# Order of the low parts at three stage changes, and the entry and head changes of the latent attention, in a two-block fp32 kernel on one core

## The chip, the core and the metric

The kernel runs on one core of a Trainium2 chip. A core has five engines that run their own instruction streams and meet at semaphores: TensorE (PE, matrix products into PSUM), VectorE (DVE), ScalarE (ACT), GpSimd (POOL) and SyncE (SP, which only issues transfers here). The metric is device microseconds of one execution; lower is better.

## What is computed

Two blocks in a row on 512 tokens of width 1024. The first has two layers: a mixer, a layer norm, a squared-ReLU MLP, a layer norm. The mixer of layer 0 is a gated delta rule, that of layer 1 a gated linear attention. The second block is a latent attention with a pooling branch.

```python
def first_block(x, ...):
    for i in range(DEPTH):                       # DEPTH = 2
        m = _mixer_gdn(x, ...) if i % 2 == 0 else _mixer_gla(x, ...)
        x = _layernorm(DEEPNORM_ALPHA * x + m, ln1_g[i], ln1_b[i])
        x = _layernorm(DEEPNORM_ALPHA * x + _sq_relu_mlp(x, mlp_w1[i], mlp_w2[i]), ln2_g[i], ln2_b[i])
    return x

# second block: h is the normed, modulated x; hc the same of the 256 context tokens
    u = h @ w_in[l];  uc = hc @ w_in[l]
    q, k, v = _mla_qkv(u, ...);  qc, kc, vc = _mla_qkv(uc, ...)   # 4 heads of 128 + 64 rotary, values 128 wide
    attn = _attend(q, concat(kc, k), concat(vc, v))               # softmax over 768 keys
    y = _branches(u, attn, w_pool[l], pool_scale[l]) @ w_out[l]   # silu gates, multiscale pooling
    x = x + gate * y
```

## The kernel before

**Large products.** Every weight and activation of the large products is split into a high part (a copy in the type fp32r, made by ACT) and a low part (the value less the high part, made by DVE). A product is then three fast products: high by high, high by low, low by high (`mm3`, L280 to L282). Weights come in slabs of 128x2048 in two halves: SP loads a half into `raw`, ACT makes `whi` (`split_hi`, L253), DVE makes `wlo` (`split_lo`, L259) and frees `raw` by the semaphore `w_ready`, on which the next load waits. PE runs one slab after another.

**The three stage changes.** The token layers `a_out`, `down0` and `b_out` each end in sums of 128 tokens (tiles 0 to 3), which must be normed and turned before `up0`, `b_qk` and `up1` can begin. DVE runs `dve_token_end`: per tile it adds the sum to `X` (L428), takes statistics (L436, L438), and, when ACT has made the root (L455, L457), centres (L447) and scales (L450) the tile, tile 3 in two halves of its columns. PE turns a tile by transposes (L395), four per half tile; ACT copies the turned half into `act_hi` (L412) and DVE subtracts it into `act_lo` (L420), both for each half tile. Before, the low parts of tile 0 stand inside tile 2's norm, those of tile 1 inside tile 3's norm (between its statistics and its centring), those of tiles 2 and 3 at the end. ACT runs `act_token_end` in a like order. PE enters the next stage in `pe_feature_first`: it waits for the low parts of tile 1, then multiplies the first two tiles with output column block 0 (`part(0, ...)`, 24 products of 256 columns), with the two half turns of tile 3 in between, then with column block 1 (another 24), and then waits for the low parts of tile 3.

**The entry of the latent attention.** At the end of `pe_c_in` six value products of 512 columns are made (L2583; each runs as two passes, so a trace has two records of it), alternately in PSUM banks 6 and 7. ACT copies the even ones out (L2715) and DVE the odd ones (L2752), so the third product waits for the copy of the first, and so on, and the first score waits for all copies. Ahead of its copies ACT runs the two halves of a `split_hi` of a slab of the last layer's weights, and DVE the two halves of its `split_lo`.

**The attention.** `pe_c_attend` makes 16 steps n, four per head, in a fixed order: the scores of step n + 1 (L2834, L2835), a piece of the preparation of the next head's keys and queries (L2600, L2604, L2590, L2595, L2608), the value product of step n - 1 (L2854), the transposes of the probabilities of step n (L2843). DVE does a step's softmax (L2972, L2974, L2976, which scales by the reciprocal), the maxima for the next (L2963, L2966), and copies turned probabilities (L2982); ACT the exponentials (L2910) and the larger copies (L2918). In the third step of a head DVE makes, after the maxima, three operands of the next head in a row: rotary queries (L2759), scaled keys `kn` (L2764), scaled rotary keys `kr` (L2765). The first score of a head waits for `kr`. POOL adds squares (L2773, L2777) and runs the pooling (L2789 to L2797) beside this.

PE's queue and all others run strictly in the order written. What is built is not chosen by a planner.

Of the kernel before, what the change touches and what calls it, by code (L numbers as in the profile page):

```python
# [16 lines left out]
ALU = mybir.AluOpType  # L17
# [91 lines left out]
def build(nc, a, out):  # L109

    ctx = ExitStack()
    with ctx:
# [134 lines left out]
        def split_hi(act, k, b):  # L247
            for hf in range(2):
                act.wait_ge(raw_loaded[hf], k * 32 + (16 * b + 16))
                if hf == 0 and not (isinstance(k, int) and k == 0):  # L250
                    act.wait_ge(slab_used, k * 2 + (b - 1))
                hs = slice(hf * SLAB // 2, (hf + 1) * SLAB // 2)
                nc.scalar.activation(whi[b][:, hs], raw[hf][:, :], ACT.Copy).then_inc(w_hi_ready, 1)  # L253
# [162 lines left out]
        def dve_turned(dve, e, st):  # L416
            for hf in range(2):
                dve.wait_ge(act_hi_ready, 8 * e + 2 * st + hf + 1)
                c = (slice(None), slice(4 * hf, 4 * hf + 4), slice(st * P, st * P + P))
                nc.vector.tensor_tensor(act_lo[c], bk[TURN_BANK[st] + hf][:, :].rearrange("p (k s) -> p k s", k=4),  # L420
                                        act_hi[c], ALU.subtract).then_inc(act_ready, 1)
# [55 lines left out]
        def act_token_end(act, name, e):  # L477
            nxt = next_pair(name, PH[name][1] // 2 - 1)
            split_first_hi(act, nxt)
            act_norm_tile(act, e, 0)  # L480
            for st in range(1, ST):
                act_norm_tile(act, e, st)
                act_turned(act, e, [st - 1])
            act_turned(act, e, [3])
            split_hi(act, nxt, 1)

        def dve_token_end(dve, name, e):
            nxt = next_pair(name, PH[name][1] // 2 - 1)
            split_first_lo(dve, nxt, [0])
            dve_norm_tile(dve, name, e, 0, lambda: split_first_lo(dve, nxt, [1]))  # L490
            dve_norm_tile(dve, name, e, 1)
            dve_norm_tile(dve, name, e, 2, lambda: dve_turned(dve, e, 0))
            dve_norm_tile(dve, name, e, 3, lambda: dve_turned(dve, e, 1))
            dve_turned(dve, e, 2)
            dve_turned(dve, e, 3)
            split_lo(dve, nxt, 1)
# [1085 lines left out]
        def pe_feature_first(pe, name, before, e, middle=None):  # L1582
# [12 lines left out]
            for hf in range(2):  # L1595
                pe.wait_ge(w_ready, 2 * PH[name][0] + hf + 1)
                part(0, range(4 * hf, 4 * hf + 4), 0, 2)
                pe_turn_half(pe, e, before, 3, hf)
            part(1, range(0, 8), 0, 2)
# [668 lines left out]
        def lst(*parts):  # L2268
# [3 lines left out]
                                  ("qt kn kr nrs", 1), ("v", 3), ("qt kn kr nrs", NH - 1)))  # L2272
# [250 lines left out]
        def pe_c_in(pe):  # L2523
# [52 lines left out]
            pe.wait_ge(V.sem, V.at("qt", 0))  # L2576
            pe.wait_ge(K.sem, K.at("lnq", 0))
            for t in range(6):
                if t in (2, 4):
                    pe.wait_ge(K.sem, K.at("v", t // 2 - 1))  # L2580
                if t in (3, 5):
                    pe.wait_ge(V.sem, V.at("v", t // 2 - 1))
                T.inc(nc.tensor.matmul(bk[6 + t % 2][:, :].rearrange("p (h n) -> p h n", h=NH), c_ckv[:, t * P:t * P + P], wv,  # L2583
                                       start=True, stop=True), "v")
            pe.wait_ge(K.sem, K.at("v", 2))
            pe.wait_ge(V.sem, V.at("v", 2))
# [69 lines left out]
        def act_c_in(act):  # L2656
# [55 lines left out]
            split_hi(act, next_pair("c_in", 3), 1)  # L2712
            for t in (0, 2, 4):
                act.wait_ge(T.sem, T.at("v", t))
                K.inc(nc.scalar.activation(c_v[:, t, :], bk[6][:, :], ACT.Copy), "v")  # L2715
# [5 lines left out]
        def dve_c_in(dve):  # L2721
# [25 lines left out]
            dve_c_keys(dve, 0)  # L2747
            dve_c_scale_column(dve, 0)
            split_lo(dve, next_pair("c_in", 3), 1)
            for t in (1, 3, 5):  # L2750
                dve.wait_ge(T.sem, T.at("v", t))
                V.inc(nc.vector.tensor_copy(c_v[:, t, :], bk[7][:, :]), "v")  # L2752
# [8 lines left out]
        def dve_c_keys(dve, g):  # L2761
            dve.wait_ge(K.sem, K.at("expk", g))
            kn, kr = HC[g % 2]["kn"], HC[g % 2]["kr"]
            V.inc(nc.vector.tensor_tensor(kn, kn, c_rsk, ALU.mult), "kn")  # L2764
            V.inc(nc.vector.tensor_tensor(kr, c_kr, c_rsk, ALU.mult), "kr")  # L2765
# [100 lines left out]
        def pe_c_attend(pe):  # L2866
            pe_c_score(pe, 0)
            for n in range(NB):
                g, qt = n // ST + 1, n % ST
                if n + 1 < NB:  # L2870
                    pe_c_score(pe, n + 1)
                if NB - ST - 1 <= n < NB - 1:
# [47 lines left out]
        def act_c_attend(act):  # L2920
            for n in range(NB):
# [6 lines left out]
                if n == NB - 1:  # L2928
                    for i in range(1, 7):
                        act_c_mix(act, i)  # L2930
                if g == NH:
                    continue
# [62 lines left out]
        def dve_c_attend(dve):  # L2995
            dve_c_max(dve, 0)
            for n in range(NB):
                g, qt = n // ST + 1, n % ST
                dve_c_softmax(dve, n)
# [4 lines left out]
                if qt == 2 and g < NH:  # L3004
                    dve_c_rope(dve, g, 7)
                    dve_c_keys(dve, g)
# [7 lines left out]
                dve_c_turned(dve, n)  # L3014
                if qt == 2 and g < NH:
                    dve_c_scale_column(dve, g)
# [168 lines left out]
```

## Time and profile before

| | us |
|---|---|
| median of 3 runs | 1873.69 |
| lowest, highest | 1873.48, 1875.39 |
| the profiled execution | 1872.41 |
| its span in the trace | 1870.4 |

| engine | busy, us | share |
|---|---|---|
| PE (matmul) | 1820.5 | 97% |
| DVE | 986.4 | 53% |
| ACT | 733.7 | 39% |
| POOL | 235.6 | 13% |

The profiled execution takes 2.0 us more than its span, and 1.3 us less than the median. In the trace's rows "idle before" stands in square brackets with what ended it. PE's clock is given as a share: 1.00 is 2.4 GHz and 0.50 is 1.2 GHz. Its mean over the span is 0.993.

### The profile page before, as it was taken

The page shows a single profiled execution, that of the slowest core. Times are in us where ns is not written, and L with a number is a line of the kernel's source. Part 1 is how long each engine was busy: PE and PEld are TensorE (multiplying, and loading weights), DVE is VectorE, ACT ScalarE, POOL GpSimd, SP SyncE. Part 2 cuts the span into 40 slices and gives each one's busy share as a digit, 9 for nine tenths or more (in the row PEclk, how much of TensorE's full clock was granted, in tenths as well). Part 3 has the DMA queues.
Part 4 walks back from the last instruction along what each step waited for, and adds up shares of the span by engine and source line. Part 5 has one row for each costly group of instructions (what it writes and reads, how often), then busy time and mean ns, then how long its engine had stood idle before and what let it go on. Part 6 is the DMA issues. An engine that isn't in the chain of part 4 may idle for free.

```text
span 1870.4 us, 24188 instructions
## 1 busy us (share of the span) xinstructions
PE 1820.5 (97%) x9152; PEld 1471.2 (79%) x9152; DVE 986.4 (53%) x1393; ACT 733.7 (39%) x1209; POOL 235.6 (13%) x230
## 2 busy tenths in 40 slices
PE   8999999999999999999999999999999998999999
PEld 6887798888788888887777787888888887875667
DVE  5775466666554453356321577744443567323663
ACT  4344455554232232333443444222223355334340
POOL 2001234342000001000000253000000000201500
PEclk9999999999999999999999999999999999999999
DMA  5323100000342234222222200442235222421001
GB/s 157 90 90 112 46 2 1 1 1 1 122 148 90 90 90 149 90 90 90 68 91 68 68 1 23 129 164 90 90 112 180 90 90 79 149 70 45 1 1 68
DMA packets 102374, 146.77 MB, mean 78 GB/s; under 512 B 4977, under 2 KB 70721, under 8 KB 102032
## 3 DMA queue, kind: packets, MB, share of 16 engines
q1 hardware_dynamic: 95472, 121.45, 20.5%
q0 software_dynamic: 6816, 24.13, 3.9%
q8 instruction: 59, 0.97, 0.2%
q14 instruction: 27, 0.22, 0.0%
HBM read 143.47 MB, written 2.10 MB: 78 GB/s over the span
## 4 chain that ended last, share of the span: by engine, by line
PE 91%; DVE 3%; issue 2%; ACT 2%; POOL 1%; DMA 1%; SPq 0%; ACTq 0%; DVEq 0%; POOLq 0%
PE bk L280 23%; PE bk L282 23%; PE bk L281 23%; PE bk L1092 2%; PE bk L1110 2%; PE bk L2834 1%; PE bk L2835 1%; PE bk L1101 1%; PE bk L2854 1%; PE bk L990 1%; POOL work L1512 1%; PE bk L1973 1%; PE bk L1008 1%; PE bk L1121 1%; PE bk L1152 1%
## 5 line engine op out<-in xcount | busy, mean ns | idle before, releaser
L259 DVE TENSOR_TENSOR wlo<-raw,whi 128x1024 fp32r<-128x1024 f32 x214 | 253.4, 1224 | 376.9 <-ACT whi L253 373.2
L280 PE MATMUL bk<-act_hi,whi 128*128 128x512 f32 x960 | 384.0, 400 | 0.3 <-DVE wlo L723 0.3
L281 PE MATMUL bk<-act_lo,whi 128*128 128x512 f32 x960 | 380.6, 396 | 0.0
L282 PE MATMUL bk<-act_hi,wlo 128*128 128x512 f32 x960 | 380.5, 396 | 0.0
L253 ACT ACTIVATE whi<-raw 128x1024 fp32r<-128x1024 f32 x214 | 216.1, 1053 | 265.5 <-PE bk L282 248.8
L280 PE MATMUL bk<-whi,act_hi 128*128 128x512 f32 x768 | 308.6, 402 | 2.5 <-DVE act_lo L473 1.8
L281 PE MATMUL bk<-wlo,act_hi 128*128 128x512 f32 x768 | 304.8, 397 | 0.0
L282 PE MATMUL bk<-whi,act_lo 128*128 128x512 f32 x768 | 304.7, 397 | 0.0
L280 PEld LDWEIGHTS bk<-act_hi,whi 128*128 128x128 f32 x960 | 180.5, 188 | 48.9 <-issue 4.1
L282 PEld LDWEIGHTS bk<-act_hi,wlo 128*128 128x128 f32 x960 | 180.5, 188 | 44.5
L281 PEld LDWEIGHTS bk<-act_lo,whi 128*128 128x128 f32 x960 | 180.6, 188 | 44.4 <-issue 1.0
L280 PEld LDWEIGHTS bk<-whi,act_hi 128*128 128x128 f32 x768 | 145.5, 189 | 38.9 <-issue 3.1
L282 PEld LDWEIGHTS bk<-whi,act_lo 128*128 128x128 f32 x768 | 145.3, 189 | 36.1
L281 PEld LDWEIGHTS bk<-wlo,act_hi 128*128 128x128 f32 x768 | 145.4, 189 | 34.6 <-issue 0.5
L1633 DVE TENSOR_TENSOR arena<-arena (+1 forms) x64 | 44.3, 692 | 182.2 <-ACT arena L1616 182.2
L1616 ACT ACTIVATE arena<-bk 128x512 f32 (+1 forms) x64 | 38.3, 598 | 245.2 <-PE bk L282 245.2
L1942 POOL TENSOR_TENSOR work<-work,arena 128x512 f32<-128x512 f32 x24 | 37.5, 1583 | 381.3 <-ACT work L1926 355.5
L473 DVE TENSOR_TENSOR act_lo<-arena,act_hi 128x2048 fp32r<-128x2048 f32 x32 | 73.3, 2292 | 18.8 <-ACT act_hi L467 18.8
L829 DVE SCALAR_TENSOR_TENSOR work<-work,convw 128x512 f32<-128x512 f32 x96 | 64.6, 743 | 0.0
L467 ACT ACTIVATE act_hi<-arena 128x2048 fp32r (+1 forms) x32 | 60.9, 1904 | 6.3 <-PE bk L282 6.3
L1092 PE MATMUL bk<-work 128*128 128x128 f32 x384 | 61.1, 280 | 1.3 <-DVE work L1433 1.2
L1440 DVE TENSOR_TENSOR work<-bk,work 128x256 f32<-128x256 f32 x96 | 40.6, 424 | 36.5 <-PE bk L1092 34.9
(392 smaller groups left out, 2500.8 us busy)
## 6 DMA issues: line engine op xcount, KB each, us to landing
raw<-in_mlp_w SPq DMA_DIRECT2D x128, 512.0 KB, 4.2
raw<-in_a_w_in SPq DMA_DIRECT2D x32, 512.0 KB, 4.0
work<-in_w_mod POOLq DMA_DIRECT2D x24, 512.0 KB, 4.1
raw<-in_b_w_in SPq DMA_DIRECT2D x24, 512.0 KB, 3.8
raw<-in_w_in SPq DMA_DIRECT2D x14, 512.0 KB, 4.0
raw<-in_a_w_out SPq DMA_DIRECT2D x8, 512.0 KB, 4.2
raw<-in_b_w_out SPq DMA_DIRECT2D x8, 512.0 KB, 4.0
raw<-in_w_out SPq DMA_DIRECT2D x8, 512.0 KB, 3.9
```

Of the source, the lines that this page charges most:

```text
L253: nc.scalar.activation(whi[b][:, hs], raw[hf][:, :], ACT.Copy).then_inc(w_hi_ready, 1)
L259: nc.vector.tensor_tensor(wlo[b][:, hs], raw[hf][:, :], whi[b][:, hs], ALU.subtract).then_inc(w_ready, 1)
L280: nc.tensor.matmul(acc, lhs_hi, rhs_hi, start=first, stop=False, skip_group_check=True)
L281: nc.tensor.matmul(acc, lhs_hi, rhs_lo, start=False, stop=False, skip_group_check=True)
L282: return nc.tensor.matmul(acc, lhs_lo, rhs_hi, start=False, stop=last, skip_group_check=True)
L467: nc.scalar.activation(stage(act_hi, b), hid_group(pair, b), ACT.Copy).then_inc(stage_hi_ready, 1)
L473: nc.vector.tensor_tensor(stage(act_lo, b), hid_group(pair, b), stage(act_hi, b), ALU.subtract).then_inc(stage_ready, 1)
L829: nc.vector.scalar_tensor_tensor(out=acc, in0=src, scalar=wk, in1=acc, op0=ALU.mult, op1=ALU.add).then_inc(conv_step, 1)
L1092: mm = nc.tensor.matmul(bk[s][:, c % 2 * P:c % 2 * P + P], A["K"][:, c, :], z_right(l, c * P, P), start=True, stop=True, skip_group_check= ...
L1440: nc.vector.tensor_tensor(A["T"][:, 2 * s:2 * s + 2, :], chunks(bk[s])[:, 0:2, :], A["negpair"][:, l, :].unsqueeze(1).broadcast_to([P, 2, ...
L1616: nc.scalar.activation(head_tile(hid, k2 * 4, 2 * b + j), bk[2 * b + j][:, :], ACT.Relu).then_inc(acc_free, 1)
L1633: nc.vector.tensor_tensor(tile, tile, tile, ALU.mult).then_inc(hid_ready, 1)
```

## The change

1. `dve_token_end` puts both low parts of tile 1 ahead of tile 3's norm, and the first low part of tile 2 inside it. `act_token_end` makes the high parts of tile 2 before the root of tile 3. `pe_feature_first` runs all of column block 0 first, and puts the two half turns of tile 3 behind the first and the second half of column block 1.
2. The six value products go to banks 2, 3, 6, 7, 4, 5, without waits for copies. The waits for the copies go to the attention's first step: for the first two copies ahead of its score of step 1, for all ahead of the next head's key product. The splits of the last layer's second slab leave the entry: each half stands at the end of an attention step, half 0 at step 3 and half 1 at step 7, on ACT and on DVE.
3. The scaling of the next head's keys, `kn`, goes ahead of the softmax of a head's third step; `kr` stays behind the rotary queries. `V`, the list of DVE's counted steps, is changed to match.

```diff
@@ act_token_end
             act_norm_tile(act, e, 0)
-            for st in range(1, ST):
+            for st in (1, 2):
                 act_norm_tile(act, e, st)
                 act_turned(act, e, [st - 1])
+            act_turned(act, e, [2])
+            act_norm_tile(act, e, 3)
             act_turned(act, e, [3])
@@ dve_token_end (dve_turned and split_hi get an argument that picks halves)
             dve_norm_tile(dve, name, e, 2, lambda: dve_turned(dve, e, 0))
-            dve_norm_tile(dve, name, e, 3, lambda: dve_turned(dve, e, 1))
-            dve_turned(dve, e, 2)
+            dve_turned(dve, e, 1)
+            dve_norm_tile(dve, name, e, 3, lambda: dve_turned(dve, e, 2, (0,)))
+            dve_turned(dve, e, 2, (1,))
             dve_turned(dve, e, 3)
@@ pe_feature_first
                 part(0, range(4 * hf, 4 * hf + 4), 0, 2)
+            for hf in range(2):
+                part(1, range(4 * hf, 4 * hf + 4), 0, 2)
                 pe_turn_half(pe, e, before, 3, hf)
-            part(1, range(0, 8), 0, 2)
@@ pe_c_in, its end
             pe_c_query_sum(pe, 0, 7)
-            pe.wait_ge(V.sem, V.at("qt", 0))
-            pe.wait_ge(K.sem, K.at("lnq", 0))
             for t in range(6):
-                if t in (2, 4):
-                    pe.wait_ge(K.sem, K.at("v", t // 2 - 1))
-                if t in (3, 5):
-                    pe.wait_ge(V.sem, V.at("v", t // 2 - 1))
-                T.inc(nc.tensor.matmul(bk[6 + t % 2][:, :].rearrange("p (h n) -> p h n", h=NH), c_ckv[:, t * P:t * P + P], wv,
+                if t == 0:
+                    pe.wait_ge(acc_free, 2 * FS["c_in"] + 16)
+                elif t == 2:
+                    pe.wait_ge(V.sem, V.at("qt", 0))
+                elif t == 3:
+                    pe.wait_ge(K.sem, K.at("lnq", 0))
+                elif t == 4:
+                    pe.wait_ge(K.sem, K.at("lnk", 1))
+                T.inc(nc.tensor.matmul(bk[V_BANK[t]][:, :].rearrange("p (h n) -> p h n", h=NH), c_ckv[:, t * P:t * P + P], wv,
                                        start=True, stop=True), "v")
-            pe.wait_ge(K.sem, K.at("v", 2))
-            pe.wait_ge(V.sem, V.at("v", 2))
+        V_BANK = (2, 3, 6, 7, 4, 5)
@@ act_c_in, its end
             act_c_query_norm(act, 0)
-            split_hi(act, next_pair("c_in", 3), 1)
             for t in (0, 2, 4):
@@ dve_c_in, its end
-            dve_c_keys(dve, 0)
+            dve_c_key_scaled(dve, 0)
+            dve_c_key_rope(dve, 0)
             dve_c_scale_column(dve, 0)
-            split_lo(dve, next_pair("c_in", 3), 1)
             for t in (1, 3, 5):
@@ pe_c_attend
                 g, qt = n // ST + 1, n % ST
+                if n == 0:
+                    pe.wait_ge(K.sem, K.at("v", 0))
+                    pe.wait_ge(V.sem, V.at("v", 0))
                 if n + 1 < NB:
                     pe_c_score(pe, n + 1)
+                if n == 0:
+                    pe.wait_ge(K.sem, K.at("v", 2))
+                    pe.wait_ge(V.sem, V.at("v", 2))
@@ act_c_attend
+                if n in (3, 7):
+                    split_hi(act, next_pair("c_in", 3), 1, (n // ST,))
                 if g == NH:
@@ dve_c_attend
+                if qt == 2 and g < NH:
+                    dve_c_key_scaled(dve, g)
                 dve_c_softmax(dve, n)
...
                 if qt == 2 and g < NH:
                     dve_c_rope(dve, g, 7)
-                    dve_c_keys(dve, g)
+                    dve_c_key_rope(dve, g)
...
                 dve_c_turned(dve, n)
+                if n in (3, 7):
+                    split_lo(dve, next_pair("c_in", 3), 1, (n // ST,))
```

**DVE at the end of `b_out`**, from the scaling of tile 2 (L450, 128x1024) to the last low parts (L420). Before:

```order
L450 SCALAR_TENSOR_TENSOR X<-X,rstd,work 128x1024
L428 SCALAR_TENSOR_TENSOR X<-X,bk 128x512
L436 BN_STATS stats<-X 128x6
L438 BN_AGGR mv<-stats 128x2
L420 TENSOR_TENSOR act_lo<-bk,act_hi 128x4x128 x2
L447 SCALAR_TENSOR_TENSOR X<-X,mv,work 128x512
L450 SCALAR_TENSOR_TENSOR X<-X,rstd,work 128x512
L447 SCALAR_TENSOR_TENSOR X<-X,mv,work 128x512
L450 SCALAR_TENSOR_TENSOR X<-X,rstd,work 128x512
L420 TENSOR_TENSOR act_lo<-bk,act_hi 128x4x128 x4
```

After:

```order
L450 SCALAR_TENSOR_TENSOR X<-X,rstd,work 128x1024
L420 TENSOR_TENSOR act_lo<-bk,act_hi 128x4x128 x2
L428 SCALAR_TENSOR_TENSOR X<-X,bk 128x512
L436 BN_STATS stats<-X 128x6
L438 BN_AGGR mv<-stats 128x2
L420 TENSOR_TENSOR act_lo<-bk,act_hi 128x4x128
L447 SCALAR_TENSOR_TENSOR X<-X,mv,work 128x512
L450 SCALAR_TENSOR_TENSOR X<-X,rstd,work 128x512
L447 SCALAR_TENSOR_TENSOR X<-X,mv,work 128x512
L450 SCALAR_TENSOR_TENSOR X<-X,rstd,work 128x512
L420 TENSOR_TENSOR act_lo<-bk,act_hi 128x4x128 x3
```

The pair of low parts of tile 1 moved up past one add and two statistics; one of tile 2's moved into the norm.

**PE at the attention's entry**: the value products, with the PSUM bank as the number behind `bk` and the semaphores waited for. Before (L2583, then the first scores):

```order
L2583 MATMUL bk6<-work,arena 128x512 [waits c_scalar,c_vector]
L2583 MATMUL bk7<-work,arena 128x512
L2583 MATMUL bk6<-work,arena 128x512 [waits c_scalar]
L2583 MATMUL bk7<-work,arena 128x512 [waits c_vector]
L2583 MATMUL bk6<-work,arena 128x512 [waits c_scalar]
L2583 MATMUL bk7<-work,arena 128x512 [waits c_vector]
L2834 MATMUL bk0<-work,arena 128x512 [waits c_vector,acc_free,c_scalar]
```

After (L2589; the score is L2841):

```order
L2589 MATMUL bk2<-work,arena 128x512 [waits acc_free]
L2589 MATMUL bk3<-work,arena 128x512
L2589 MATMUL bk6<-work,arena 128x512 [waits c_vector]
L2589 MATMUL bk7<-work,arena 128x512 [waits c_scalar]
L2589 MATMUL bk4<-work,arena 128x512 [waits c_scalar]
L2589 MATMUL bk5<-work,arena 128x512
L2841 MATMUL bk0<-work,arena 128x512 [waits c_vector,c_scalar,acc_free]
```

Each product now has a bank of its own; the waits left are for other readers of those banks.

**DVE in a head's third attention step** (n = 2). Before, from the copy of step 1's turned probabilities (L2982) to that of step 2:

```order
L2982 COPY arena<-bk 128x256
L2972 TENSOR_TENSOR arena<-arena 128x1
L2974 RECIPROCAL arena<-arena 128x1
L2976 TENSOR_SCALAR work<-work,arena 128x768
L2963 TENSOR_REDUCE arena<-bk 128x1 x2
L2966 TENSOR_SCALAR arena<-arena 128x1
L2759 TENSOR_TENSOR work<-bk,work 128x512
L2764 TENSOR_TENSOR work<-work 128x768
L2765 TENSOR_TENSOR work<-arena,work 128x768
L2982 COPY arena<-bk 128x256
```

After:

```order
L2997 COPY arena<-bk 128x256
L2769 TENSOR_TENSOR work<-work 128x768
L2987 TENSOR_TENSOR arena<-arena 128x1
L2989 RECIPROCAL arena<-arena 128x1
L2991 TENSOR_SCALAR work<-work,arena 128x768
L2978 TENSOR_REDUCE arena<-bk 128x1 x2
L2981 TENSOR_SCALAR arena<-arena 128x1
L2764 TENSOR_TENSOR work<-bk,work 128x512
L2772 TENSOR_TENSOR work<-arena,work 128x768
L2997 COPY arena<-bk 128x256
```

`kn` (L2764 before, L2769 after) moved from the front of `kr` to the front of the softmax.

## Rows read from the trace of the kernel before

**Rows 1.** Waits of PE: total us, times, longest.

```profile
PE bk L280 <- issue: 5.9, 3, 2.1
PE bk L280 <- DVE act_lo L2396: 4.1, 1, 4.1
```

**Rows 2.** Timeline of PE at the three stage changes: start us, us, operation.

```profile
517.25 0.36 PE L280 MATMUL bk<-act_hi,first_hi 128*128 128x256 f32 x1 [1.82 <-issue]
...
890.24 0.35 PE L280 MATMUL bk<-act_hi,first_hi 128*128 128x256 f32 x1 [2.08 <-issue]
...
1203.99 1.09 PE L395 MATMUL bk<-eye,X 128*128 128x128 f32 x8
1207.06 0.36 PE L280 MATMUL bk<-act_hi,first_hi 128*128 128x256 f32 x1 [1.98 <-issue]
...
1210.44 0.60 PE L395 MATMUL bk<-eye,X 128*128 128x128 f32 x4
```

**Rows 3.** Timeline of DVE at the third of them.

```profile
1202.65 1.28 DVE L450 SCALAR_TENSOR_TENSOR X<-X,rstd,work 128x1024 f32<-128x1024 f32 x1
...
1205.72 1.23 DVE L420 TENSOR_TENSOR act_lo<-bk,act_hi 128x512 fp32r<-128x512 f32 x2
...
1209.77 2.63 DVE L420 TENSOR_TENSOR act_lo<-bk,act_hi 128x512 fp32r<-128x512 f32 x4
```

**Rows 4.** Timeline of all engines at the attention's entry.

```profile
1699.73 0.95 PE L2608 MATMUL bk<-ones,arena 128*128 128x2 f32 x8
...
1702.15 0.95 DVE L2765 TENSOR_TENSOR work<-arena,work 128x768 f32<-128x768 f32 x1
...
1703.09 2.35 DVE L259 TENSOR_TENSOR wlo<-raw,whi 128x1024 fp32r<-128x1024 f32 x2
...
1703.98 1.12 PE L2583 MATMUL bk<-work,arena 128*128 128x512 f32 x2 [0.57 <-ACT arena L2715]
...
1706.10 3.03 PE L2583 MATMUL bk<-work,arena 128*128 128x512 f32 x6 [1.00 <-DVE arena L2752]
...
1709.97 1.10 PE L2834 MATMUL bk<-work,arena 128*128 128x512 f32 x2 [0.83 <-issue]
```

**Rows 5.** Timeline at the changes to heads 1 and 2.

```profile
1728.34 1.02 PE L2834 MATMUL bk<-work,arena 128*128 128x512 f32 x2
...
1728.67 0.16 DVE L2972 TENSOR_TENSOR arena<-arena 128x1 f32<-128x1 f32 x1 [1.52 <-ACT work L2910]
...
1730.91 1.50 PE L2854 MATMUL bk<-arena 128*128 128x128 f32 x12
...
1732.36 1.57 DVE L2764 TENSOR_TENSOR work<-work 128x768 f32<-128x768 f32 x1
...
1733.20 1.86 POOL L2797 TENSOR_TENSOR arena<-arena 128x512 f32<-128x512 f32 x1
...
1733.42 0.85 PE L2843 MATMUL bk<-eye,work 128*128 128x128 f32 x6
...
1733.86 2.01 DVE L2765 TENSOR_TENSOR work<-arena,work 128x768 f32<-128x768 f32 x1
...
1736.13 2.04 PE L2834 MATMUL bk<-work 128*128 128x512 f32 x2 [1.86 <-DVE work L2765]
...
1741.38 1.05 PE L2854 MATMUL bk<-arena 128*128 128x128 f32 x5
...
1764.50 0.85 PE L2843 MATMUL bk<-eye,work 128*128 128x128 f32 x6
1766.98 1.10 PE L2834 MATMUL bk<-work,arena 128*128 128x512 f32 x2 [1.63 <-ACT arena L2918]
```

**Rows 6.** Table by stretch: us; busy us (instructions) of PE, PEld, DVE, ACT, POOL; PEclk, DMA share, GB/s.

```profile
1585.10:1588.40 3.30, 3.30 (x18) 3.30 (x17) 2.56 (x6) 3.30 (x8) 0.00 (x0) 0.50 0.41 110
...
1735.30:1742.00 6.70, 5.87 (x11) 3.47 (x12) 4.04 (x8) 0.50 (x2) 5.11 (x4) 0.50 0.00 0
...
1203.00:1210.00 7.00, 5.02 (x38) 4.39 (x37) 6.64 (x11) 1.98 (x5) 1.05 (x2) 1.00 0.41 140
```

More of the change, by code:

```diff
@@ L245, in load_slab, with split_hi @@
                              ).then_inc(raw_loaded[hf], 16)
-        def split_hi(act, k, b):
-            for hf in range(2):
+        def split_hi(act, k, b, parts=(0, 1)):
+            for hf in parts:
                 act.wait_ge(raw_loaded[hf], k * 32 + (16 * b + 16))
@@ L414, in act_turned, with dve_turned @@
                                          ACT.Copy).then_inc(act_hi_ready, 1)
-        def dve_turned(dve, e, st):
-            for hf in range(2):
+        def dve_turned(dve, e, st, halves_of=(0, 1)):
+            for hf in halves_of:
                 dve.wait_ge(act_hi_ready, 8 * e + 2 * st + hf + 1)
@@ L2271, in build @@
         V = Steps("c_vector", lst(("ga1 ga", 1), ("stats stats mean ms", 2), ("lo", 8), ("lo tmp lo", 8), ("gate gst gg tabq lat lat tk tk lat", 1),
-                                  ("qt kn kr nrs", 1), ("v", 3), ("qt kn kr nrs", NH - 1)))
+                                  ("qt kn kr nrs", 1), ("v", 3), ("kn qt kr nrs", NH - 1)))
         K = Steps("c_scalar", lst(("ln rs xn", 2), ("tmp hi", 8), ("square ln rs diag", 3), ("tmp hi hi", 1),
@@ L2711, in act_c_in @@
             act_c_query_norm(act, 0)
-            split_hi(act, next_pair("c_in", 3), 1)
             for t in (0, 2, 4):
                 act.wait_ge(T.sem, T.at("v", t))
-                K.inc(nc.scalar.activation(c_v[:, t, :], bk[6][:, :], ACT.Copy), "v")
+                K.inc(nc.scalar.activation(c_v[:, t, :], bk[V_BANK[t]][:, :], ACT.Copy), "v")
         def act_c_pin(act, b, j):
@@ L2746, in dve_c_in @@
             dve_c_rope(dve, 0, 6)
-            dve_c_keys(dve, 0)
+            dve_c_key_scaled(dve, 0)
+            dve_c_key_rope(dve, 0)
             dve_c_scale_column(dve, 0)
-            split_lo(dve, next_pair("c_in", 3), 1)
             for t in (1, 3, 5):
                 dve.wait_ge(T.sem, T.at("v", t))
-                V.inc(nc.vector.tensor_copy(c_v[:, t, :], bk[7][:, :]), "v")
+                V.inc(nc.vector.tensor_copy(c_v[:, t, :], bk[V_BANK[t]][:, :]), "v")
         def dve_c_rope(dve, g, bank):
@@ L2759, in dve_c_rope, with dve_c_key_scaled, dve_c_key_rope @@
             V.inc(nc.vector.tensor_tensor(HB[g % 2]["qt"], bk[bank][:, :], CW["tabq"], ALU.mult), "qt")
-        def dve_c_keys(dve, g):
+        def dve_c_key_scaled(dve, g):
             dve.wait_ge(K.sem, K.at("expk", g))
-            kn, kr = HC[g % 2]["kn"], HC[g % 2]["kr"]
+            kn = HC[g % 2]["kn"]
             V.inc(nc.vector.tensor_tensor(kn, kn, c_rsk, ALU.mult), "kn")
-            V.inc(nc.vector.tensor_tensor(kr, c_kr, c_rsk, ALU.mult), "kr")
+        def dve_c_key_rope(dve, g):
+            V.inc(nc.vector.tensor_tensor(HC[g % 2]["kr"], c_kr, c_rsk, ALU.mult), "kr")
         def dve_c_scale_column(dve, g):
```

## The prediction

> **What bounds the kernel now.** The table of busy times comes first: PE is busy for 1820.5 of 1870.4 us, so only two things shorten the kernel: less time in which PE stands still, and less time at its lower clock. The waits of PE say where it stands still. Its largest entry is three waits "issue" of about 2 us each, in which the profile sees no partner [rows 1]. The timeline of PE puts them at the first product of each of the three stage changes [rows 2]. The timeline of DVE beside it names the partner: at the third change the low parts of tile 1 end at 1205.72 + 1.23 = 1206.95 and PE starts at 1207.06 [rows 2, 3]. A second place is the attention's entry, from 1700.7 to 1709.97, where PE stands between its value products for copies [rows 4]. A third is the first score of heads 1 and 2, which waits 1.86 and 1.63 us for what DVE does [rows 5]. The largest single wait, 4.1 us at `c_in`'s own entry [rows 1], isn't touched. Last comes the table by stretch, for the clock: the stretch behind head 1's wait has 0.50 [rows 6].
>
> **Stage changes.** At the third one DVE has tile 2 scaled at 1202.65 + 1.28 = 1203.93 [rows 3]. Put right behind it, tile 1's pair of low parts (1.23) ends at about 1205.2, and PE starts at 1205.3 in place of 1207.06: 1.75 gained. That is 0.23 less than the idle time of 1.98 there, and I take 0.23 off the other two as well: 1.6 and 1.85 [rows 2]. Together 5.2.
>
> What is late next? The low part of tile 3's last half. From its turn's start at 1210.44 to its low part's end at 1209.77 + 2.63 = 1212.40 it takes 1.96 [rows 2, 3]. Before, 24 products of column block 1 covered that. Now the last turn stands behind them, and the cover is the turn itself and 12 products of block 0. From PE's start to its last turn there were 24 products and a half turn in 3.38 us (1207.06 to 1210.44), so 12 products are some 1.4 and a half turn 0.4 to 0.5: cover 1.85 against 1.96 plus 0.1 for the semaphore. I charge 0.2 at each change, 0.6 in all. The turns themselves find their data: PE now reaches the last one 1205.3 + 3.4 + 2.9 = 1211.6; DVE's norm of tile 3 starts 1.2 later than before but has lost one of the two low parts that stood in it, and ends its last scaling about half a microsecond later, near 1210.3. ACT's high parts of tile 2 are ready before the root of tile 3 is wanted, so that swap is free. **Net 4.6.** Bounds: 5.9 if the whole idle time goes, 2.8 if the last half costs 0.8 at each. Behind it the next slab's low parts (two of 1.2) come about 1.1 us later, near 1216.2; PE wants them when the first slab's 96 products (11.3 us, by 1.4 for 12) and the half turns are through, near 1217.6, so that costs nothing, with little over 1 us to spare.
>
> **The entry.** PE's last sum ends at 1699.73 + 0.95 = 1700.7 [rows 4]. Six value products follow. Three of them with two waits in between took 3.03; two passes without a wait are 1.02 to 1.12 with the last one's tail, 0.86 from start to start [rows 4, 5]. So six take 5.2 bare, 6.0 with waits as in the row; I take 5.6, and the first score starts at 1706.3 in place of 1709.97: **3.7**, with bounds of 3.3 and 4.1. What could hold it is ready: `kr` is ready at 1702.15 + 0.95 = 1703.1, the values' copies are no longer waited for until the scores of step 1 (2.6 later), and each copy is some 0.6 to 0.7 behind its product. The two halves of low parts that stood ahead of DVE's copies, 2.35 us [rows 4], are gone from there.
>
> **The heads.** In head 1's case DVE makes `kn` from 1732.36 for 1.57 and then `kr` for 2.01; PE is through with the transposes at 1733.42 + 0.85 = 1734.27 [rows 5]. With `kn` gone `kr` takes its slot and ends at 1733.93 if it takes `kn`'s time, 1734.4 if it takes its own. So PE starts at about 1734.2 in place of 1736.13: 1.9 (1.7 at the worse price). Head 2 has the same pattern, 1766.98 against 1764.50 + 0.85: 1.6. Head 3 waits a few tenths, which no row here carries; I take 0.3. **Sum 3.8**, bounds 3.2 and 4.1. `kn` itself now stands where DVE was idle for 1.52 us before the softmax [rows 5]; without POOL beside it such an operation takes 0.95 (the `kr` there) [rows 4], so it is covered. If the cover fails, the softmax is late by at most 0.95, and PE wants its result only after scores and a value product.
>
> Both take 1.57 and 2.01 in place of 0.95 while POOL works, and POOL's own L2797 takes 1.86 there [rows 5]. The Trainium skill, "SBUF — State Buffer", section "SBUF: two separate sides", says that VectorE and GpSimd share one port pair, held by one instruction at a time while the other fully blocks. By that rule `kr` in the earlier slot ends with the POOL operation that runs at its start, plus its own length, as `kn` did: 1733.9, the better end of my bounds; by its own measured 2.01 the sum would be 0.4 smaller over two heads.
>
> **The splits that moved.** Two ACT halves and two DVE halves (1.2 each [rows 4]) go into steps 3 and 7. These steps have no key work. What stands behind DVE's half is the next step's softmax, for whose result PE makes a score (2.6) [rows 5], a key product and a value product first. At step 7 POOL's pooling runs, and half and softmax can each be stretched; I charge 0.2 in all, bounds 0 and 1.5. The halves free `raw`, and so SP's next two loads of the last layer start 35 and 70 us later than before. They are wanted only when the last layer is under way, far later than the 4 us that such a load takes.
>
> **The clock.** The stretch from 1735.30 has 0.50, which is 1.2 GHz [rows 6]. Before it PE had stood still for 1.86 us, after a stretch of short transposes [rows 5]. A score and all that belongs to it took 2.6 us at full clock (1728.34 to 1730.91) and 5.25 at the lower one (1736.13 to 1741.38) [rows 5]; with the value product's share behind it the loss is **3.0**. I take it that without the wait the clock stays up.
>
> The waits of about 2 us at the stage changes did not lower the clock: 1.00 around the third [rows 6]. The Trainium skill, "TensorE: Matmul & The Clock Gate", section "What's actually happening", says that the gate's watch runs freely and doesn't start with the kernel. By that rule the same wait can cost 3.0 in one run and nothing in another, so the gain isn't certain in the median, and another wait (the 4.1 at `c_in`, behind which 3.3 us stand at 0.50 [rows 6]) can cost 1.6 more or less. The forecast without that gain is the first rival.
>
> **Sum.** 4.6 + 3.7 + 3.8 - 0.2 + 3.0 = 14.9. The profiled execution took 1872.4, so 1857.5; the median of the runs is 1.3 above it, which gives **1858.8**.
>
> **Rivals.**
> - *The clock isn't won* (the lower stretch comes elsewhere in the attention, or before's runs didn't have it): 11.9 gained, 1861.8. For it: full clock behind two like waits. Against: the drop follows the longest wait of the attention at once. 0.27.
> - *A new wait at the stage changes*: if the chain turn, copy, low part of the last half comes out longer than 1.96, since ACT and DVE have both become later, each change gives back 1 us or more: 2 gained of 4.6, 1861.4. The cover is 1.85 and has no slack. 0.10.
> - *DVE is the limit in the attention*: the softmax at steps 4 and 8 is late behind the moved halves and POOL, 1 us each, and heads' gains shrink by 1: 1861.8. 0.08.
> - *Slower*: the attention's steps stay at 1.2 GHz. Its many short products are what ran before the one drop; each further drop of that size costs 3.0, so six of them over the attention's 110 us turn 14.9 into a loss (1862 + 15 = 1877). Before had one. 0.02.
> - *It does not do what it says*, the waits being for something that the trace doesn't show (they are called "issue"): all but the entry stays, 1870 or more. The end of the low parts 0.11 us ahead of PE's start speaks against it. 0.03.
>
> The forecast has 0.50. The range: the favourable ends (stage changes +1.3, entry +0.4, heads +0.3, no drop at `c_in` +1.6) give 1855.2, the first three rivals and their mixtures reach 1864: **1854.8 to 1864.3**. The measurement can tell about 0.2%, 3.7 us. Faster by more than that: 0.95; within: 0.03; slower: 0.02.
>
> **What would show it.** At the three changes PE's idle time before the first product falls to 0.2 to 0.5, and a wait of 0.1 to 0.3 appears before the products of tiles 2 and 3. From PE's last sum to the first score 5.6 us (9.3 before), with no gap over 0.2 between value products. Before the first scores of heads 1 and 2 no wait over 0.3. No stretch at 0.50 in the attention. The forecast is wrong if `kr` grows with POOL beyond 2.0, if a low part of tile 3 is waited for by more than 0.5, or if a stretch at 0.50 stands anywhere new.

## The result and the profile after

The changed kernel takes 1854.63 us (median of four runs, 1850.26 to 1858.02) where the kernel before takes 1874.45 (1873.48 to 1875.39): a ratio of 0.9893 with a 95% interval of 0.9871 to 0.9915, or 19.8 us. The forecast was 1858.8 with a range of 1854.8 to 1864.3. The direction was right. The time is 4.2 us below the forecast and 0.2 below the range; the gain is 19.8 us (15.9 to 24.2 by the interval) where 14.9 was forecast. The profiled execution took 1850.26, with a span of 1848.3 against 1870.4.

The waits of PE (total us, times, longest), which answer to [rows 1]. The entry "issue" has shrunk from 5.9 to 0.5, and the wait at `c_in` is what it was:

```profile
PE bk L280 <- DVE act_lo L2400: 4.2, 1, 4.2
...
PE bk L280 <- issue: 0.5, 3, 0.2
```

The third stage change, timeline of PE and then of DVE; it answers to [rows 2, 3]:

```profile
1198.32 1.09 PE L395 MATMUL bk<-eye,X 128*128 128x128 f32 x8
1199.57 0.36 PE L280 MATMUL bk<-act_hi,first_hi 128*128 128x256 f32 x1 [0.15 <-issue]
...
1205.76 0.60 PE L395 MATMUL bk<-eye,X 128*128 128x128 f32 x4
...
1208.90 0.28 PE L282 MATMUL bk<-act_hi,first_lo 128*128 128x256 f32 x1
1209.02 0.28 PE L280 MATMUL bk<-act_hi,first_hi 128*128 128x256 f32 x1
```

```profile
1196.98 1.28 DVE L450 SCALAR_TENSOR_TENSOR X<-X,rstd,work 128x1024 f32<-128x1024 f32 x1
1198.18 1.28 DVE L420 TENSOR_TENSOR act_lo<-bk,act_hi 128x512 fp32r<-128x512 f32 x2
...
1204.44 1.44 DVE L420 TENSOR_TENSOR act_lo<-bk,act_hi 128x512 fp32r<-128x512 f32 x2
1207.03 0.69 DVE L420 TENSOR_TENSOR act_lo<-bk,act_hi 128x512 fp32r<-128x512 f32 x1 [1.15 <-ACT act_hi L412]
```

From the last full turn to the first product there are now 1199.57 - 1198.32 = 1.25 us, before 3.07 [rows 2]: 1.82 gained. At the first change it is 517.25 - 514.34 = 2.91 before and 516.62 - 515.38 = 1.24 after, at the second 890.24 - 887.13 = 3.11 and 884.53 - 883.34 = 1.19: **5.4** in all. The low part of tile 3's last half ends at 1207.03 + 0.69 = 1207.72, and PE wants it at 1209.02: no wait. Tile 3's first half has less to spare: its low part is the second of the pair that ends at 1204.44 + 1.44 = 1205.88, and PE wants it at 1206.12.

The entry and the first scores of the heads, timeline of PE (entry, then head 1, head 2, head 3) and, of all engines, DVE's `kn` and `kr` of head 1 with the POOL operation beside `kr`; they answer to [rows 4, 5]:

```profile
1688.84 0.95 PE L2614 MATMUL bk<-ones,arena 128*128 128x2 f32 x8
1689.65 5.40 PE L2589 MATMUL bk<-work,arena 128*128 128x512 f32 x12
1694.88 1.02 PE L2841 MATMUL bk<-work,arena 128*128 128x512 f32 x2
```

```profile
1718.26 0.85 PE L2850 MATMUL bk<-eye,work 128*128 128x128 f32 x6
1719.05 1.10 PE L2841 MATMUL bk<-work 128*128 128x512 f32 x2
...
1744.49 0.85 PE L2850 MATMUL bk<-eye,work 128*128 128x128 f32 x6
1745.28 1.10 PE L2841 MATMUL bk<-work,arena 128*128 128x512 f32 x2
...
1770.73 0.85 PE L2850 MATMUL bk<-eye,work 128*128 128x128 f32 x6
1771.42 1.02 PE L2841 MATMUL bk<-work 128*128 128x512 f32 x2
```

```profile
1712.21 0.96 DVE L2769 TENSOR_TENSOR work<-work 128x768 f32<-128x768 f32 x1 [0.21 <-ACT work L2653]
...
1716.89 1.09 POOL L2801 TENSOR_TENSOR arena<-arena,work 128x512 f32<-128x512 f32 x1
1717.20 1.59 DVE L2772 TENSOR_TENSOR work<-arena,work 128x768 f32<-128x768 f32 x1
```

From the last sum to the first score 1694.88 - 1688.84 = 6.04 us, before 1709.97 - 1699.73 = 10.24 [rows 4]: **4.2**. From the turns to a head's first score 0.79 us at heads 1 and 2, before 2.71 and 2.48 [rows 5], and 0.69 at head 3, before 1793.45 - 1792.43 = 1.02: 1.92 + 1.69 + 0.33 = **3.9**. Together the three places give 13.5 us of shorter waits, and 19.8 were measured. The other 6.3 have no wait to belong to.

The table by stretch shows where they are (us, busy us of PE, PEld, DVE, ACT, POOL, PEclk, DMA share, GB/s). In this execution the lower clock stands in two places only besides the end:

```profile
211.60:215.01 3.41, 3.41 (x17) 3.41 (x17) 1.07 (x3) 1.67 (x5) 3.41 (x4) 0.50 0.00 0
1573.52:1576.93 3.41, 2.84 (x13) 2.87 (x14) 2.70 (x5) 3.31 (x10) 0.00 (x0) 0.50 0.15 17
```

The kernel before had 3.4 us at `c_in`, 6.8 at head 1's wait [rows 6], and 6.8 at each of the two modulation steps, which the prediction did not look at. Such a step is 32 passes of two columns, 3.5 us from start to start at full clock; the clock falls 2.7 and 2.5 us after its start. The first step in PE's timeline, and both stretches in the table:

```profile
698.28 4.34 PE L1677 MATMUL bk<-ones,work 128*128 128x2 f32 x32
```

```profile
701.00:707.80 6.80, 6.80 (x22) 5.64 (x22) 3.79 (x4) 1.77 (x1) 4.81 (x8) 0.50 0.60 184
1390.50:1397.30 6.80, 6.80 (x23) 5.74 (x23) 4.36 (x6) 1.98 (x2) 1.42 (x2) 0.50 0.64 226
```

A stretch at half clock costs half its length where PE is busy throughout, and less where it waits, so by this estimate these executions lost at most 11.9 and 3.4 us. The changed kernel's four runs had mean clocks of 0.998, 0.996, 0.995 and 0.993 and took 1850.26, 1854.21, 1855.05 and 1858.02. A difference of 0.005 in the mean clock over 1850 us is 9 us (an estimate), so the spread of 8 us goes with the clock.

### The profile page after: what moved, and what is told of

It is laid out like the page before. It is cut to its first block, busy times and chain, and to the rows that moved or that the text cites. A ratio compares the mean times of both kernels' runs of the same rounds, so it can differ in the third digit from the quotient of the medians.

```text
span 1848.3 us, 24188 instructions
## 1 busy us (share of the span) xinstructions
PE 1810.2 (98%) x9152; PEld 1465.5 (79%) x9152; DVE 987.5 (53%) x1393; ACT 735.3 (40%) x1209; POOL 235.4 (13%) x230
## 4 chain that ended last, share of the span: by engine, by line
PE 92%; DVE 2%; ACT 2%; issue 2%; POOL 1%; DMA 1%; SPq 0%; ACTq 0%; DVEq 0%; POOLq 0%
PE bk L280 23%; PE bk L282 23%; PE bk L281 23%; PE bk L1095 2%; PE bk L1113 2%; PE bk L1104 1%; PE bk L2841 1%; PE bk L2842 1%; PE bk L2861 1%; PE bk L993 1%; POOL work L1515 1%; PE bk L1977 1%; PE bk L1011 1%; PE bk L1124 1%; PE bk L1155 1%
```

## The experiments

All times are medians; ratios are of this kernel to the kernel before, run on the same chip, with 95% intervals. There the kernel before took 1873.1 in the first group (runs 1 to 4) and 1872.3 in the other two, with runs from 1866 to 1877.

**1. The stage changes alone**: the hunks on `dve_turned`, `act_token_end`, `dve_token_end` and `pe_feature_first`.

> The kernel before with the edits of the three stage changes alone. Theory A (the waits removed are the gain, and the clock's stretches at 0.50 stay where the kernel before had them): idle time before the first product falls from 1.98, 2.24 and 2.14 to some 0.3 at each, no wait before tiles 2 and 3, so 5.5 us less than the kernel before: a median near 1869, and stretches at 0.50 behind both modulation steps, at the last layer's entry and in the attention. Theory B (the place of each stretch at 0.50 goes by the phase of a watch that runs on its own, and a low-activity stretch of 3.5 us such as the modulation step is hit or missed with the shift): same mechanical 5.5, but with stretches missing or added, each worth 3.4, so anything from 1866 to 1872 and runs that differ by steps of 1.7 to 3.4. Rival of the prediction (a new wait for tile 3's last low part): 3 us less at most, 1871.5.

Measured: 1862.9 (1858.41 to 1866.21), ratio 0.9945 (0.9929 to 0.9961), 10.3 us. The rows give 5.4 us from the waits, as in the changed kernel. That leaves 4.9 for the clock (1.9 to 7.9 by the interval), and the median is below what either theory gave: both took the waits' own share alone, or with a few stretches shifted. Its profile has 0.50 in five places before PE's end, 3.4 us at the first modulation step and 6.8 at the second, so the places are theory B's.

**2. The heads alone**: `dve_c_keys` parted in two, `kn` ahead of the softmax.

> The kernel before with the head change alone (kn ahead of the softmax, kr in its slot). Theory A: the waits of 2.02, 1.79 and 0.33 us before the first scores of heads 1 to 3 go, 4.1, and with them the stretch at 0.50 that follows the first, 3.0 to 3.4: 7.3 in all, a median near 1867. Theory B (that stretch goes by the phase of a free-running watch): 4.1 in every run, and the stretch in the attention gone or not, others as before: 1867 to 1870.5.

Measured: 1866.53 (1863.85 to 1869.90), ratio 0.9973 (0.9964 to 0.9981), 5.1 us: 3.9 from the waits, about 1 from the clock, where the prediction had 3.0. The time is near both theories' numbers, the places are theory B's. The profile holds the row that the prediction was wrong on. These are stretches of this kernel; its stage changes are those of the kernel before, and behind the second and third of them the clock is down:

```profile
890.00:893.41 3.41, 3.41 (x19) 3.41 (x18) 3.38 (x6) 0.60 (x1) 0.00 (x0) 0.50 0.02 5
1207.44:1210.85 3.41, 3.41 (x17) 3.41 (x17) 3.34 (x6) 0.00 (x1) 0.53 (x1) 0.50 0.38 120
...
698.00:708.00 10.00, 10.00 (x62) 8.72 (x61) 7.06 (x7) 4.49 (x5) 3.80 (x7) 1.00 0.35 97
```

The waits in front of them are the old ones of 2.0 us; the first modulation step, which starts at 700.2 in this run and has 6.8 us of lower clock at it in the kernel before, has none here.

**3. The entry alone**: `V_BANK`, the waits, and the two pairs of halves moved.

> The kernel before with the attention's entry alone (six value products in banks of their own, the two pairs of halves moved to steps 3 and 7). Theory A: 4.4 us from the last sum to the first score, less up to 0.3 for the moved halves; the wait before head 1's first score stays at 2.0 and with it the stretch at 0.50: 1870.2. Theory B: the same 4.4, and the stretch behind head 1's wait, now 4.4 us earlier in the phase of the watch, may be shorter or gone: down to 1867. Rival (the moved halves make the softmax of steps 4 and 8 late): waits of PE of 1 us each there, 1872.

Measured: 1868.33 (1866.55 to 1872.89), ratio 0.9974 (0.9963 to 0.9984), 4.9 us, against 4.2 in the rows, between theories A and B. No wait appears at the softmax of steps 4 and 8: the moved halves cost nothing. Its profile fell into a long execution (1872.89) with eight stretches at 0.50 before PE's end, behind all three stage changes, both modulation steps, the waits at 207 and at `c_in`, and head 1. Two of them:

```profile
519.17:522.58 3.41, 3.41 (x18) 3.41 (x17) 3.34 (x6) 0.60 (x1) 0.53 (x1) 0.50 0.36 88
703.49:710.31 6.82, 6.82 (x24) 5.85 (x24) 4.23 (x4) 2.20 (x2) 4.01 (x7) 0.50 0.57 176
```

The three parts by themselves give 10.3 + 5.1 + 4.9 = 20.3 us, together 19.8. Within their intervals they add up, and no part needs another.

**4. The modulation products spread** over the next layer's first slab pair, in the changed kernel. The call is shown; `pe_mod_column` makes two of the products at each call, and the old loop over them goes.

```
-pe_token_slab(pe, name, half, 0, b, pair0, b == 0, False)
+pe_token_slab(pe, name, half, 0, b, pair0, b == 0, False,
+              (lambda pe, st, b=b: pe_mod_column(pe, int(name[-1]), 4 * b + st)) if half == 0 else None)
```

> The changed kernel with the two modulation steps (16 products of 2 columns each, 3.5 us of PE with next to no columns) taken apart: two of them behind each of the eight tiles of the down layer's first slab pair. The products are the same. Theory A (the spread of the changed kernel's runs, 1850.3 to 1858.0, is the stretches at 0.50 behind the modulation steps, there in some runs and not in others): with 0.45 us holes only, no stretch follows them, so all runs lie near 1850 to 1851 and differ by less than 2. Theory B (the spread comes from other places, the entries of the two attentions): the runs spread as before, 1850 to 1858, and the median stays near 1854.6. Taking them apart itself should cost or gain under 0.5, since the load of weights sets the pace in both.

Measured: 1868.10 (1866.95 to 1870.49), ratio 0.9975 (0.9966 to 0.9984): some 15 us slower than the changed kernel. Both theories missed it. DVE waits for the modulation sum before it goes on to the next low parts, so with the products finished 20 us later DVE stood still for 20 us and PE then for it, timeline of DVE and of PE:

```profile
723.46 0.17 DVE L1693 TENSOR_TENSOR modc<-bk,cols 128x16 f32<-128x16 f32 x1 [20.21 <-PE bk L311]
```

```profile
728.67 0.80 PE L280 MATMUL bk<-whi,act_hi 128*128 128x512 f32 x1 [5.24 <-DVE act_lo L483]
```

The run says nothing on the clock question, which run 6 puts in another way.

**5. PE kept busy in the stage changes' waits** of the kernel before.

```
+for i in range(2):
+    nc.tensor.matmul(bk[6][:, :], eye[:, :], X[:, 2, 512 * i:512 * i + 512], ...)
 pe.wait_ge(acc_free, 2 * FS[name] - 2)
 pe.wait_ge(act_ready, 8 * e + 4)
```

> The kernel before, with two extra products (eye by a tile of X, 512 columns, about 1.7 us of PE together, result never read) put into the wait of 2 us at each of the three stage changes. The wait for DVE stays as it is; only PE isn't idle in it. Theory A (the stage-change edits gained 10.2 us where 5.5 of idle time went, because an idle time of 2 us there is, in a part of the runs, followed by 3.4 us at half clock): 3 to 5 us less than the kernel before, a median near 1869.5, no stretch at 0.50 behind a stage change. Theory B (the rest of the gain is something else that the new order brings, say a better start of the new stage): the same time as the kernel before, within 1 us.

Measured: 1869.27 (1865.86 to 1873.45), ratio 0.9987 (0.9975 to 1.0000), 2.4 us, or 3.0 between medians. At the third stage change, timeline of PE, the extra products are those of L1594:

```profile
1200.72 1.06 PE L395 MATMUL bk<-eye,X 128*128 128x128 f32 x8
1201.62 1.88 PE L1594 MATMUL bk<-X,eye 128*128 128x512 f32 x4
1203.84 0.36 PE L280 MATMUL bk<-act_hi,first_hi 128*128 128x256 f32 x1 [0.33 <-issue]
```

From the last full turn to the first product it is still 3.07, 3.12 and 3.12 us, so no first product comes earlier. The profile has no stretch at 0.50 behind a stage change. It leans to theory A, but the interval touches no gain. Run 12 fills these waits together with all others, so what the stage changes alone carry rests on this run and on the counts below.

**6. The modulation products 128 columns wide**, in the kernel before. The operand of ones has 128 columns; each later product overwrites what isn't wanted.

```
-bk[4][:, 4*n + 2*w : 4*n + 2*w + 2], mod_acc[:, w, n*P : n*P + P], ones[:, 0:2]
+bk[4][:, 4*n + 2*w : 4*n + 2*w + P], mod_acc[:, w, n*P : n*P + P], ones[:, :]
```

> The kernel before, with the products of the two modulation steps 128 columns wide in place of 2 (the operand of ones is taken whole, each later product overwrites the columns that aren't wanted). One product of two passes takes 0.22 us with 2 columns, the pace of the weight loads, and 128 columns pass in 0.22 too: the step stays at 3.5 us. Theory A (the stretch of 3.5 us with next to no columns is what the stretches at 0.50 behind it come from, two in the profile of the kernel before, 6.8 us each): both go in all runs, 3.4 us less for each where it stood: a median of 1867 to 1869. Theory B (the drop there has another reason): 1873.

Measured: 1867.86 (1865.79 to 1872.14), ratio 0.9980 (0.9970 to 0.9990), 3.7 us. The step takes as long as with two columns (3.49 us from start to start), and the clock stays up at both of them. A timeline row, and then stretches of this kernel:

```profile
699.21 3.73 PE L1677 MATMUL bk<-ones,work 128*128 128x128 f32 x32
```

```profile
697.00:708.00 11.00, 11.00 (x66) 9.52 (x65) 7.06 (x7) 4.49 (x5) 4.70 (x8) 1.00 0.35 115
1386.00:1398.00 12.00, 12.00 (x70) 10.34 (x69) 8.11 (x9) 4.89 (x5) 1.43 (x2) 1.00 0.35 118
```

With wide products the stretches at these steps are gone, as theory A says, and the time is in its range, though the table counts PE as busy throughout in either form.

**7. The changed kernel again.**

> The changed kernel once more, for the spread of its runs and a second profile. Theory A (the places of the stretches at 0.50 go by a phase that each run has of its own): median 1852 to 1856, a spread of some 8 us, and stretches in the profile at other places than at 211.6 and 1573.5, above all behind the modulation steps. Theory B (they are fixed to the program): the same two stretches and the same 1850 in most runs.

Measured: 1851.99 (1851.76 to 1855.44), ratio 0.9898 (0.9883 to 0.9914). The stretches in its profile stand at 702.2 (at the first modulation step's end, 3.4 us) and at `c_in`, not at 211.6:

```profile
702.20:705.61 3.41, 3.41 (x10) 2.64 (x9) 2.55 (x3) 0.53 (x1) 3.11 (x6) 0.50 0.81 262
...
207.20:214.00 6.80, 4.04 (x21) 2.41 (x20) 4.89 (x7) 4.93 (x12) 1.09 (x2) 1.00 0.44 154
```

The same program, other places: theory A for the places. Five of its six runs lie within 0.9 us, so the spread was narrower than expected. This second median is 2.8 us below the range.

The start of the program is one more place. In this profile the products of 512 columns take 0.63 us or more each up to some 16 us and 0.4 after that; in the first profile it is 0.4 from 11.2 us on, and the product of `eye` by `work` (L701) comes at 19.01 in place of 20.86. Of the 14 profiles three are like that (runs 2, 7 and 9), and the table by stretch doesn't show it.

**8. The changed kernel kept warm**: run 6's edit, four products of `eye` by `X` in the wait at `c_in`, two by the keys in the wait at 207.

> The changed kernel with the modulation products 128 columns wide, and PE kept at work in its two longest waits: four extra products of eye by X (3.4 us) in the wait of 4.3 at the last layer's entry, two by the keys (1.7 us) in the wait of 2.6 behind the first key turns. Nothing waits for less. Theory A (what is left of the stretches at 0.50 follows these four places): none left but the one behind the last product, a median near 1847 and a spread below 2. Theory B (other places take them over, as the waits of 1.3 to 1.5 us at 456, 1045 and 1052): one or two stretches stay, 1849 to 1853.

Measured: **1847.76** (1847.47 to 1848.02), ratio 0.9873 (0.9857 to 0.9889), mean clock 1.000 in all five runs. It is 4.2 us faster than the changed kernel on the same chip (run 7), the fastest of all versions here; the extra products' results are never read. Theory A's signs are all there.

**9. DVE's and ACT's new order alone**, PE's old one.

> The kernel before with the new order of DVE and ACT at the three stage changes, and PE's old one (tile 3's first half turn behind 12 products of column block 0, the second behind 24). Theory A (both halves of the edit are needed, since DVE ends tile 3's two scalings some 1.2 us later): at the third change PE starts 1.8 earlier, reaches tile 3's first turn after 1.4 us, 2.0 before it is there, and stands still there: the idle time has moved by 12 products and the median stays within 1 us of the kernel before. Theory B (the order of DVE alone brings the gain): 5 us of mechanical gain, 10 in the median, as with the whole edit.

Measured: 1871.34 (1868.78 to 1873.02), ratio 0.9992 (0.9982 to 1.0001). The wait has moved, as theory A says; waits of PE:

```profile
PE bk L395 <- DVE X L450: 5.7, 3, 1.9
```

**10. PE's new order alone.**

> The kernel before with PE's new order at the three stage changes and DVE's and ACT's old one. Theory A: the first product still waits 2.0 to 2.2 us for tile 1's low parts, and nothing else was waited for, so the time is that of the kernel before within 0.5 us and the same spread. Theory B (the later turn of tile 3 makes its low parts late, as the prediction held): 0.2 to 0.8 us lost at each change, up to 2 us slower.

Measured: 1872.83 (1866.25 to 1876.20), ratio 1.0001 (0.9988 to 1.0013), the waits those of the kernel before:

```profile
PE bk L280 <- issue: 6.0, 3, 2.1
```

No loss clear of the noise, and no wait before tile 3's products: PE's later turn of tile 3 does not by itself bring the wait that the prediction charged. Runs 9 and 10 together: neither half of the edit brings a gain clear of the noise without the other.

**11. Run 6's edit alone in the changed kernel.**

> The changed kernel with the modulation products 128 columns wide and nothing else. Theory A (they are one of the two places where runs of the changed kernel lose half-clock stretches; the waits at 207 and 1570 are the other): between the changed kernel (1852 to 1854.6) and the one with all four places kept busy (1847.8): 1850 to 1852, at least one stretch of 3.4 us behind the wait at the last layer's entry. Theory B (the modulation steps cost nothing there): 1852 to 1855.

Measured: 1851.45 (1850.83 to 1851.61), ratio 0.9888 (0.9872 to 0.9904), within theory A's numbers. Between the medians of runs 7 and 8 lie 4.2 us; this edit brings 0.5 of them, which the intervals can't tell from nothing. The rest is put down to the waits at 207 and at `c_in`, where its profile has stretches of 3.4 and 6.8; no run parts these two.

**12. The kernel before kept warm**: runs 5's, 6's and 8's products, and two more before the first scores of heads 1 and 2.

> The kernel before with PE kept at work in its long waits: extra products of eye by X in the three stage changes' waits, the last layer's entry, the waits before the first scores of heads 1 and 2 and behind the first key turns, and the modulation products 128 columns wide. No wait of before is shorter. It parts the change's gain in two: against the changed kernel treated so (1847.8) it shows what the shorter waits alone bring. Theory A (13.5 to 14 us from waits, 5 to 7 from the clock): 1861.5 to 1863, a spread below 2, no stretch at 0.50 but the last. Theory B (the extra gain is not the clock's): 1867 or more, since the waits make 14 of 20.

Measured: **1861.29** (1860.99 to 1861.69), ratio 0.9942 (0.9925 to 0.9958), mean clock 0.999 or 1.000, 0.2 below theory A's numbers. This parts the gain. Both kernels kept warm: 1861.29 - 1847.76 = **13.5 us, the shorter waits**, the very sum of the rows (5.4 + 4.2 + 3.9). The two ran on different chips; there the kernel before took 1872.28 and 1872.30. The kernel before loses 1872.3 - 1861.3 = 11.0 us to the clock; the changed one loses 4.2 (run 7) to 6.9 (its first four runs). The difference, 4 to 7 us, is the clock's part of the gain.

A second witness needs no extra products: the mean clock of every run. A run's span times what its mean clock lacks to 1 gives an estimate of the loss. The means over all executions, beside the kernel before on the same chip:

| | loss to the clock, us | before, us |
|---|---|---|
| changed kernel, first four runs | 8.3 | - |
| changed kernel, run 7 | 5.6 | 12.0 |
| run 1, stage changes | 8.7 | 13.2 |
| run 2, heads | 11.4 | 13.2 |
| run 3, entry | 12.7 | 13.2 |
| run 5, stage changes' waits filled | 8.7 | 12.0 |
| run 6, wide modulation products | 8.2 | 12.0 |
| run 8, changed, kept warm | 0.0 | 12.0 |
| run 12, before, kept warm | 0.7 | 12.8 |

In runs 1, 2, 3, 5 and 6 what the clock gave back by this table and the shortened waits together come within 0.9 us of the measured gain.

## Why the prediction was wrong, point by point

- **Stage changes**: first products 5.2 earlier forecast, 5.4 measured. The 0.6 charged for the low part of tile 3's last half was a slip: the cover was put at "12 products of block 0", but the loop in `pe_feature_first` issues both blocks' first halves, 24 products, before it touches the last half of the slab. From the turn at 1205.76 to 1209.02 there are 3.26 us of cover, not 1.85, against a chain of 1.96, as forecast. Net 5.4 in place of 4.6. The rival built on it (0.10) took the wrong half: it is tile 3's first half that is close, with a cover of 1206.12 - 1203.91 = 2.21 and 0.24 to spare.
- **Entry**: 4.2 in place of 3.7, above its bounds. The products run at 0.44 from start to start, twelve passes 5.23; the 5.6 kept a share for waits, none of which was left.
- **Heads**: 3.9 in place of 3.8. `kr` in `kn`'s slot took 1.59 beside POOL, which is `kn`'s old 1.57 and not its own 2.01. What the Trainium skill says in "SBUF — State Buffer", section "SBUF: two separate sides", agrees roughly: POOL's operation beside `kr` ends at 1716.89 + 1.09 = 1717.98, `kr`'s own length of 0.95 behind that gives 1718.93, and it ended at 1717.20 + 1.59 = 1718.79. `kn` without POOL took 0.96, and stands in idle time.
- **Moved halves**: 0.2 charged, no wait of PE found.
- **The clock**: 3.0 forecast, 6.3 measured (19.8 - 13.5; between 2.4 and 10.7 by the interval alone, and 4 to 7 by runs 7, 8 and 12). This is the term that failed: it makes 3.3 of the 4.9 us by which the gain was forecast too small. Its step was "The waits of about 2 us at the stage changes did not lower the clock: 1.00 around the third", with head 1's stretch as the only one to win. Counting over the profiles of all these kernels, with one execution each: behind the unchanged wait at a stage change the lower clock stood 7 times of 15 (none in the kernel before and run 10, two in runs 2 and 6, three in run 3); where the wait was gone 0 times of 18, where it was filled 0 of 6. Behind head 1's old wait it stood in 6 of 7, for 3.9 us on average, worth 1.9 and not 3.0. At two-column modulation steps, from within the step or up to 1.4 us behind it, 12 times of 18, at wide ones never in 8. At `c_in` always, 12 of 12, and behind the wait at 207 6 of 12, unless filled; the change leaves both as they were. Behind head 2's old wait, 1.63 us, it stood in none of 7. So the stage changes carried by estimate 7/15 x 3 x 1.7 = 2.4 us of clock on average beside head 1's 1.9.
- The rest, some 2 us, is not shown. The counts point at the modulation steps: 11 of 14 of them have lower clock in the kernel before and runs 1, 2, 3, 5, 9 and 10, 1 of 4 in the changed one (run 7 and the first profile). Whether that comes from the shift of what stands ahead or from few samples was not told apart.
- **The range** failed by the same step. Its favourable end counted 1.6 for `c_in` and nothing for the modulation steps, two of the trace's three longest stretches. The reason to count them was in the text: by the Trainium skill, "TensorE: Matmul & The Clock Gate", section "What's actually happening", the watch runs freely, and the prediction applied that to the gain but not to the waits that happened to escape in the one execution it had. Runs 2, 3 and 7 agree with the rule: the same waits and steps are followed by lower clock in one execution and not in another.
- **The rivals**: none of them happened. The clock was won, no new wait stands at the stage changes, no wait for the moved halves appears in the attention, and the "issue" waits fell to 0.15 us with the new order of DVE and ACT alone (run 9), so they were for these two.
- **Expected signs**: idle time before the first products 0.15 to 0.2, a little under the forecast; 5.1 us from the last sum's end to the first score (5.6 forecast); no wait before heads 1 and 2; no 0.50 in the attention. The wait of 0.1 to 0.3 before tiles 2 and 3 did not appear, and "a stretch at 0.50 anywhere new" did, at 211.6.

## What to carry to other kernels

Read the clock from several executions, or count for each wait of TensorE what stands behind it in some of them: a wait that kept its clock in one trace has only escaped once. Part the waits from the clock by a version that does idle work in each wait; its runs agree here within 0.7 us, and the changed kernel in that form is the fastest version. When a consumer's wait is removed by reordering the producer, look at what the producer now delivers later, and move the consumer's order with it: neither half alone gained anything clear of the noise.

## What the runs showed of the hardware

- An idle time of 2 us of TensorE at a stage change was followed by a clock of 0.50 in about half of the cases (7 of 15); the 4.2 us at `c_in` every time (12 of 12), the 1.63 us before head 2 never (0 of 7).
- A step of 3.5 us that counts as fully busy, but passes two columns a product, came with up to 6.8 us at half clock in 12 of 18 cases. With 128 columns it took the same time, 3.49 us, and no such stretch came (0 of 8).
- With its waits filled, the runs of the kernel before agree within 0.7 us (1860.99 to 1861.69); as it was, they lie between 1866 and 1877.
